# LayerNorm stage of a two-layer decoder step: statistics, powers and scalings taken in one iteration, group by group, and the second pointwise weights begun within the convolution

## The reference, cut to what matters

```python
def conv_module(h, past, w_pw1, b_pw1, w_dw, b_dw, ln_g, ln_b, w_pw2, b_pw2):
    a, gate = jnp.split(h @ w_pw1 + b_pw1, 2, axis=-1)
    u = a * jax.nn.sigmoid(gate)
    u_ext = jnp.concatenate([past, u], axis=1)
    c = lax.conv_general_dilated(u_ext, w_dw[:, None, :], ...) + b_dw   # causal depthwise, width 31
    c = jax.nn.silu(layer_norm(c, ln_g, ln_b))                          # over the 1024 channels
    return c @ w_pw2 + b_pw2, u_ext[:, -CONV_CTX:]
...
    h = h + y                                   # h1
    hn = rms_norm(h, norm_ffn[i])
    y = swiglu(hn, ffn_w_gate, ffn_w_up, ffn_w_down)
```

## Time and profile before

| | |
|---|---|
| median of 3 runs | 2887.03 us (2877.52, 2887.03, 3138.01) |
| profiled execution | 2906.26 us; span 2904.8 us on its slowest core, core 6 |
| spans of the 8 cores | 2860.2 to 2904.8 us |
| PE, DVE, ACT, POOL busy | 85%, 33%, 26%, 20% of the span |
| the LayerNorm stage on core 6 | first scaling 266 us, last turn 401 us |

### The profile page before, as it was taken

The page is one execution under the profiler, slowest core; times in us unless marked ns, Lnnn a source line. Parts: engine busy times, 40 slices in busy tenths (PEclk is TensorE's granted clock), DMA queues, the critical chain, the costliest instruction groups (busy, mean ns, idle before and its releaser), DMA issues. The chain is left out here.

```text
span 2904.8 us, 43996 instructions; the slowest of 8 cores (2860.2 to 2904.8 us)
## 1 busy us (share of the span) xinstructions
PE 2456.1 (85%) x18993; PEld 1697.5 (58%) x19081; DVE 958.0 (33%) x1466; ACT 767.8 (26%) x1117; POOL 576.5 (20%) x830
## 2 busy tenths in 40 slices
PE   4894788889799937768529999999999999999666
PEld 2453344445344414434328899887789888888532
DVE  4464641112133315667512121211122211112166
ACT  4212531111122226657311121111122111111154
POOL 1002520000000025455321111111112111110152
PEclk8886899999899968889769999999999999999889
DMA  7536426663322264131478999988899999984363
GB/s 192 109 77 120 149 79 145 150 155 98 70 70 70 69 153 112 55 111 61 111 154 145 146 193 177 166 147 150 129 158 173 184 170 181 162 154 78 99 174 116
DMA packets 137498, 378.45 MB, mean 130 GB/s; under 512 B 31192, under 2 KB 41544, under 8 KB 136048
## 3 DMA queue, kind: packets, MB, share of 16 engines
q0 software_dynamic: 69648, 233.80, 47.6%
q1 hardware_dynamic: 67648, 141.76, 15.1%
HBM read 513.69 MB, written 77.39 MB: 203 GB/s over the span
## 5 line engine op out<-in xcount | busy, mean ns | idle before, releaser
L550 PE MATMUL pb<-arena 128*128 128x0 bf16 x7168 | 793.9, 274 | 0.8 <-DVE arena L511 0.8
L550 PEld LDWEIGHTS pb<-arena 128*128 128x128 bf16 x7168 | 674.8, 98 | 116.7 <-issue 1.1
L578 PE MATMUL pb<-arena 128*128 128x0 bf16 x3584 | 404.9, 274 | 0.0
L558 DVE TENSOR_TENSOR arena<-arena,pb 128x640 bf16<-128x640 f32 x224 | 184.0, 821 | 652.3 <-PE pb L550 652.3
L578 PEld LDWEIGHTS pb<-arena 128*128 128x128 bf16 x3584 | 336.0, 98 | 56.5
L1448 PE MATMUL pb<-arena 128*128 128x413 bf16 (+1 forms) x1760 | 322.3, 347 | 33.8 <-DVE arena L1455 33.8
L557 ACT ACTIVATE arena<-pb 128x640 f32<-128x640 f32 x224 | 157.5, 703 | 620.6 <-PE pb L550 620.6
L1448 PEld LDWEIGHTS pb<-arena 128*128 128x128 bf16 x1760 | 175.0, 100 | 179.9 <-DVE arena L1455 36.6
L1012 PE MATMUL pb<-arena 128*128 128x128 bf16 (+1 forms) x1180 | 100.1, 239 | 158.5 <-ACT arena L1359 38.4
L149 POOL DMA_DIRECT2D arena<-moe_gu x224 | 118.8, 534 | 566.5 <-PE pb L550 270.2
L1012 PEld LDWEIGHTS pb<-arena 128*128 128x128 bf16 (+1 forms) x1180 | 79.0, 108 | 195.1 <-ACT arena L1359 44.1
(11 more groups left out here) (209 smaller groups left out, 2327.4 us busy)
## 6 DMA issues: line engine op xcount, KB each, us to landing
arena<-moe_gu POOLq DMA_DIRECT2D x224, 512.0 KB, 8.2
arena<-moe_d POOLq DMA_DIRECT2D x128, 448.0 KB, 10.0
arena<-x SPq DMA_DIRECT2D x32, 512.0 KB, 7.1
arena<-ffn_gu POOLq DMA_DIRECT2D x22, 512.0 KB, 6.8
XG<-arena SPq DMA_DIRECT2D x4, 2560.0 KB, 13.2
arena<-XG SPq DMA_DIRECT2D x8, 1280.0 KB, 31.8
YD<-arena SPq DMA_DIRECT2D x8, 1280.0 KB, 15.6
h1D<-arena SPq DMA_DIRECT2D x16, 512.0 KB, 3.6
```

The costliest lines, as they stand in the source:

```text
L550: last = e.matmul(bank(b + h, HALF).shape_from_register(sr), w[:, a, kc, :], xg[:, kc, h * HALF:(h + 1) * HALF].shape_from_register(sr), s ...
L558: S.op("dve", lambda e: e.tensor_tensor(out=self.hx[:, f, :].rearrange("p (h c) -> p h c", h=2), in0=sg, in1=self.two(bU), op=ALU.mult), r ...
L578: last = e.matmul(bank(b + h, HALF).shape_from_register(sr), w[:, k, :], self.hx[:, f, h * HALF:(h + 1) * HALF].shape_from_register(sr), s ...
```

## The change

W2's load goes from behind the convolution to the start of its loop's iteration c = 4, ahead of uout(4). x2_load is cut into the load and x2_bias, the addition on POOL. In the LayerNorm loop the iteration now takes, in this order: the statistics of pA; the turns and silus of pB; ln_z of pA (before: of pB, at the top); then for each tile of pD its pw2, the h1_scale of the tile of pE that goes with it, h1_add, the x load of t+3, the turn and copy of the tile of pE, and h1_sq; and at the end the additions of b2 for both tiles.

```diff
     for c in range(8):
+        if c == 4:
+
+            w2_holder.append(A.new(O_W1, [128, 8, D], BF16))
+            S.dma("pool", w2_holder[0][0].rearrange("p k d -> p (k d)"), w2, "w2", w=[w2_holder[0][1]])
 
         uout(c)
...
-    W2, W2_r = A.new(O_W1, [128, 8, D], BF16)
-    S.dma("pool", W2.rearrange("p k d -> p (k d)"), w2, "w2", w=[W2_r])
+    W2, W2_r = w2_holder[0]
...
         S.dma("sp", b[0:n, :], xph[t] if t < 16 else xs[:, :], sem, w=[r_])
+        x2t[t] = (b, r_)
+
+    def x2_bias(t):
+        n = rowsof(t)
+        b, r_ = x2t[t]
         S.op("pool", lambda e: e.tensor_tensor(out=b[0:n, :], in0=b[0:n, :], in1=b2[0:n, :], op=ALU.add), r=[b2_r], w=[r_])
-        x2t[t] = (b, r_)
...
-        zs = [ln_z(t) for t in pB]
-        xs2 = [h1_scale(*sqs.pop(t)) for t in pE]
-        if pD:
-            zT, zT_r = zts.pop(pD)
-            bk = pw2(pD[0], zT, zT_r, 0)
-            h1_add(pD[0], bk)
+        for t in pA:
+            ln_stat(t)
         if pB:
             zts[pB] = ln_b(pB, zs)
-        for v in xs2[0:1]:
-            xturn2(*v)
-        if pD:
-            sqs[pD[0]] = h1_sq(pD[0])
-        if len(pD) > 1:
-            bk = pw2(pD[1], zT, zT_r, 1)
-        for v in xs2[1:]:
-            xturn2(*v)
-        for t in pA:
-            ln_stat(t)
-        if len(pD) > 1:
-            h1_add(pD[1], bk)
-            sqs[pD[1]] = h1_sq(pD[1])
+        zs = [ln_z(t) for t in pA]
+        xs2 = []
+        for j, t in enumerate(pD):
+            if j == 0:
+                zT, zT_r = zts.pop(pD)
+            bk = pw2(t, zT, zT_r, j)
+            xs2.append(h1_scale(*sqs.pop(pE[j]))) if pE else None
+            h1_add(t, bk)
+            if t + 3 < NB:
+                x2_load(t + 3)
+            if pE:
+                xturn2(*xs2[j])
+            sqs[t] = h1_sq(t)
+        for t in pE[len(pD):]:
+            xturn2(*h1_scale(*sqs.pop(t)))
         for t in pD:
             if t + 3 < NB:
-                x2_load(t + 3)
+                x2_bias(t + 3)
```

More of the change, by code:

```diff
@@ L1290, in build @@
     consts_more()
+    w2_holder = []
     for c in range(8):
+        if c == 4:
+            w2_holder.append(A.new(O_W1, [128, 8, D], BF16))
+            S.dma("pool", w2_holder[0][0].rearrange("p k d -> p (k d)"), w2, "w2", w=[w2_holder[0][1]])
         uout(c)
@@ L1461, in build @@
         x2_load(t)
+    for t in range(3):
+        x2_bias(t)
+    zs = []
     zts, sqs = {}, {}
```

## The result

| | before | after |
|---|---|---|
| median of 8 runs | 2882.78 us | 2902.53 us (2897.87 to 2915.05) |
| ratio of the times, 95% interval | | 1.0076 [1.0046, 1.0107] |
| spans of the 8 cores in the profile | 2860.2 to 2904.8 us | 2875.6 to 2899.7 us |
| the stage, median of 8 cores | 166.3 us (165.5 to 170.3) | 185.65 us (185.3 to 189.0) |

The change makes the kernel slower by 0.76%, some 22 us (13 to 31); the forecast was 2901. The ratio leaves out disturbed executions, such as those of before near 3130 us.

The account below looks back on a forecast made before the run. No engine full in the 228 to 401 us stretch; the program behind is PE-bound, so changes count one to one. +1.7 + 8.5 + 4.5 = +14.7 us on the 2887.03 median gave 2901, range 2868 to 2928.

Parts of the forecast that it names:

- start, to the first scaling: Convolution end to first LayerNorm scaling: W2's earlier load brings everything up to the first silu 9.2 us earlier.
- first pass, to h1_add of tile 1: First pass of the new LayerNorm order: h1_add of tile 1 at 276.9 instead of 283.94, -7.0 us.
- crowded pair, to h1_add of tile 3: x loads queued behind five ffn_gu loads: h1_add of tile 3 at 301.5 against 299.83, +1.7 us, start's lead gone.
- five iterations: LayerNorm loop, h1_add of tile 3 to tile 13: 86.1 us against 77.6, +8.5; bounds +2 and +16.
- end: From h1_add of tile 13 to the last turn: 28.2 us against 23.7, +4.5, possibly 2.
- the cycle: LayerNorm loop: closed chain from one second tile's h1_add through x load, addition, powers and pw2 to the next, 17.4 us.
- T as the next bound: Last convolution chunk: with the U load early, matmuls wait for DVE's building of T and start near 238.2, not 250.06.
- SP's state stores: SP queue at the convolution's end: two state stores take 0.8 us in place of 9.46, x loads issued 9.2 earlier.
- The rival that the move gains nothing: Convolution end: last U load late for another reason, lead of 9.2 missing, up to +24 us, 2911; chance 0.06.
- slower still: LayerNorm loop: x loads land at 5.9 us and pw2 stays at 5.2, in all +22 us, 2909; chance 0.15.
- The faster rival: LayerNorm loop: x lands in 3.4 us, POOL's gate opens 1.6 earlier, cycle 14.9, in all -7.5 us, 2879; chance 0.16.
- the additions' gate: POOL in the LayerNorm loop: powers stand behind b2 additions that wait for x, part of the 17.4 us chain.

Follow-up runs that it names:

- Kernel 1: The kernel before with only W2's load moved to c = 4 of the convolution, old LayerNorm order kept; ratio to before 0.9985, stage 159.45 us.
- kernel 2: The changed kernel with W2's load put back behind the convolution, new order kept; ratio to before 1.0097, stage 194.1 us.
- Kernel 3: The changed kernel with POOL's b2 additions put behind the next iteration's statistics and powers; ratio to before 1.0011, stage about 172 us.
- kernel 5: The changed kernel with the first b2 addition at the iteration's end, the second behind the next iteration's first h1_sq; ratio to before 1.0002, stage 168.3 us.
- kernel 6: The changed kernel with b2 added by a ninth PE matmul per pw2 half instead of on POOL; ratio to before 0.9945, median 2870.33 us.
- Kernel 9: kernel 5 with both pw2 of an iteration issued before its turns; ratio to before 0.9957, stage 158.2 us.

## Why the prediction was right, and where its terms were off

The forecast was 2901 and the measured median 2902.53. The mechanism was right; that the number is so near is in part luck. The forecast is +14.7 us on a median of three, 2887.03; the eight executions of before have 2882.78, and the change is some 22 us (13 to 31). So the base was some 4 us too high and the change some 7 too small. The terms, by the parts of the prediction (the first two are steps on the way to the third, and the last three make the sum):

| term | forecast | between the two profiled cores | medians over the cores |
|---|---|---|---|
| start, to the first scaling | -9.2 | -8.9 | -8.6 |
| first pass, to h1_add of tile 1 | -7.0 | -7.4 (45.8 against 53.2) | -7.1 |
| crowded pair, to h1_add of tile 3 | +1.7 | -0.4 | -0.9 |
| five iterations | +8.5 (86.1) | +11.35 (88.93) | +17.4 (92.0 against 74.6) |
| end | +4.5 (28.2) | +4.2 (27.85) | +4.1 |
| sum | +14.7 | +15.1 | +19.4 |

The two profiled cores flatter the forecast. Core 6 of before has the longest five iterations of its eight (77.58 us, the others 72.8 to 75.8), core 5 of after the shortest (88.93, the others 89.2 to 93.0). By the medians the cycle cost twice what the forecast gave it.

**The start** was right in mechanism and size: U load, T as the next bound, SP's state stores, x landing 8.2 us behind its issue (219.70 to 227.89), where I had kept 8.4. Kernel 1 shows it by itself. The rival that the move gains nothing also stated what the order alone would cost, up to +24; kernel 2 has +27.8.

**The crowded pair** was near: after the ffn_gu issue at 241.12 the additions start at 263.79, 22.7 us on and not 26.2 as before. The whole lead of 9 us goes there, as forecast.

**The cycle.** The mis-sized term is pw2. The iteration from 332.12 has: issue of x 0.40, landing 4.38 (forecast 5.0), addition 2.34, powers and -mu*rstd 2.10, h1_scale 1.20, to PE 0.05, turn 0.83 (0.45), pw2 to h1_add 5.29 (4.5 and 0.07), h1_add 1.23. Sum 17.82, forecast 17.4. So the load was 0.6 us faster, and what hangs on PE behind its gap 1.1 slower: turn +0.38, pw2 +0.7. I had put pw2 between the row without a gap, 3.62, and the slow one, 4.90; the second pw2 of the steady iterations took 4.5 to 5.9 on this core and up to 6.2 on others. The rival "slower still" had the right pw2 (5.2) with the wrong landing (5.9); the two misses here have opposite signs. That makes 17.8 as the mean of the five on core 5, the lowest of the eight cores (up to 18.6), against a forecast of 17.2. The iterations of 19 us and more, one or two of the five on every core, all have a second pw2 of 5.6 to 6.2 us, and several an x that lands up to 1.8 us behind the first addition.

**The faster rival** could not have come true in this order. POOL has two additions, and the chain of the forecast counts one: the first runs from 335.46 to 337.81, behind the power of a square, and x of the second lands 0.3 us later. With x landed in 3.4 us the gate would have opened 0.3 us sooner here, and 0.8 at the mean of the 40 iterations of the eight cores, not the 1.6 that the rival takes.

**The end** came to its number partly by a term I didn't have: an h1_scale of 3.42 us at 373.14, beside the second of the additions at 370.81. The kernel before had the same conflict, which I took no note of: on core 6 two powers on POOL (289.54 and 305.36) take 1.45 and 1.43 us beside an h1_scale, and 0.57 elsewhere.

**What the forecast would not have given** is the cure. The links of its chain were named, but I held the additions' gate to be all that the new order had to lose. Kernel 3 took the gate away and got back 13.7 of an expected 35 us, because the same additions also block DVE there; kernel 5 avoided that too and was left with a pw2 of 6.17 us at a low clock. With the additions gone (kernel 6) the gain of the new order appears. Kernel 9 keeps them, and its time can't be told from kernel 6's (0.9957 against 0.9945), though its stage is 10.8 us longer.

## What to carry to other kernels

An in-order queue that mixes work for now with work for later is read for what the *later* one waits on: here a bias addition that waits for a load, harmless at the queue's end, became a gate for the whole stage when urgent powers were put behind it. Before moving such an operation, ask whether it can leave the engine altogether: a K = 1 matmul in an accumulation that exists anyway removed the load's gate and the port conflict at once. And price an operation by its rows at the clock that it will have behind its new gap, not by its best row.

## What the runs showed of the hardware that I had not expected

**A VectorE operation that reads two tiles of SBUF stands still beside POOL's additions, even for one element per partition**: 2.29 us in place of 0.16, and 3.44 in place of 1.28, let go by the end of an addition; 0.21 with one SBUF input. A forecast that puts such an operation and POOL side by side as independent is off by up to the whole POOL instruction, 2.3 us here.

**PE's clock comes back late.** The windows of the changed kernel around one gap (columns as in kernel 5's window):

```profile
333.16:336.78 3.62, 3.62 (x19) 1.48 (x16) 3.52 (x7) 3.30 (x6) 2.08 (x3) 1.00 0.71 222
336.78:343.82 7.04, 0.00 (x0) 0.00 (x1) 1.76 (x6) 4.43 (x6) 4.94 (x6) 0.79 0.09 35
343.82:344.65 0.83, 0.83 (x8) 0.83 (x9) 0.83 (x1) 0.20 (x1) 0.00 (x0) 0.50 0.00 0
344.65:347.64 2.99, 2.99 (x10) 1.06 (x9) 2.17 (x3) 1.15 (x2) 1.17 (x2) 0.50 0.64 200
347.64:349.94 2.30, 2.30 (x16) 1.24 (x15) 0.00 (x1) 0.00 (x0) 0.00 (x0) 0.98 0.52 196
```

The first pw2 runs at a granted clock of 1.00 (2.4 GHz) in 3.62 us; PE then idles for 7.04 us, and the clock falls within that gap; the turn and most of the second pw2 run at 0.50 (1.2 GHz), and only the last 2.3 us are back at 0.98. The length of the gap alone doesn't set the price: in kernel 6 a gap of a quarter of that is followed by a stretch of work nearly as long at the low clock (windows of kernel 6, core 3):

```profile
254.00:255.60 1.60, 0.00 (x0) 0.00 (x0) 1.37 (x2) 1.50 (x4) 0.15 (x1) 1.00 0.93 335
255.60:259.50 3.90, 3.89 (x16) 1.59 (x16) 3.01 (x3) 3.61 (x5) 0.20 (x1) 0.56 0.63 188
259.50:262.20 2.70, 2.70 (x14) 1.05 (x14) 0.00 (x0) 0.00 (x0) 0.58 (x2) 1.00 0.77 159
```

There the fall comes only when PE is back at work. So kernel 6's 13.4 us still hold some 1.5 us of a slow pw2; an iteration without any gap on PE wasn't reached in this study.

**A ninth matmul of one partition is cheap**: 0.39 us recorded for 1x128 by 1x512, twice per tile, where POOL's addition of the same bias took 2.34 us and could hold DVE as long.
